# Second RMS norm of a decoder layer: squares behind the output projection, token-major sums, and the first FFN blocks by k tile

## The chip, the core and the metric

The kernel runs on one core of a Trainium2 chip. The metric is the time of the whole kernel on the device, in microseconds (us), median of several runs. Engines: TensorE (PE in the profile, its weight loads PEld), VectorE (DVE), ScalarE (ACT), GpSimd (POOL), and SyncE (SP), which here issues most of the DMAs. TensorE's clock has two levels, 1.2 and 2.4 GHz; the profile gives the granted clock as a share of the higher.

## The reference

One layer of a hybrid decoder trunk, on x of 1024 tokens by 1024 channels, float32. What matters here is the end of the layer:

```
mixed = (gate_a * o_a + gate_b * o_b + gate_c * o_c) @ w_out
x  = x + g1 * mixed
h2 = rms_norm(x) * (1 + sc2) + sh2          # x * rsqrt(mean(x*x, over channels) + 1e-6)
gate, up = split(h2 @ w_ffn_in, 2)          # D_FF = 2816
x  = x + g2 * ((silu(gate) * up) @ w_ffn_out)
```

Before it stand a first adaLN norm, one wide input projection and three branches (RG-LRU, RWKV-7, sliding-window attention), which the change doesn't touch.

## The kernel before

**Layout.** Activations are channel-major: a k tile is 128 channels on the partitions and 1024 tokens in the free dimension, so x is eight k tiles (`x2`). The names T and D are 1024, KT is 8, P is 128. Sums over channels are sums over partitions and over k tiles, and are done by TensorE.

**Dense products.** Every matrix product runs on float32 split in two parts, high and low: weights in `w_hi`, `w_lo`, activations in `x_hi`, `x_lo`. `dense` takes one block, 128 output channels: for each k tile `three_passes` issues hi*hi, hi*lo, lo*hi on two halves of 512 tokens, six matmuls (L246). A block's result lies in two of the eight PSUM banks, chosen by its slot (0 or 1; banks 0 and 1, or 2 and 3). The weights of all blocks form one stream with two slots. SP loads a block's raw weights (`load_block`, L228) once the block two before it has been split. POOL splits it (`split_block`, a cast at L236 and a subtraction at L238) once the raw weights have landed and the block two before, which has the same slot, is done on TensorE. TensorE waits for the split.

**Order.** No planner: each engine runs its own written program in order, and semaphores join them. A helper `upto(n)` turns "n events done" into a wait. SP's queue is in order too, so a load that waits holds back every load written behind it.

**The merge and x.** The last branch product (`ob1`) leaves the merged activations in `mix`; ScalarE rounds them to `x_hi` (L1349), VectorE makes `x_lo` (L1830). x, which comes token-major from memory, is loaded again in eight tiles of 128 tokens into two slots of `yraw` (L580 to L585) and transposed by TensorE (L1025 to L1031) into banks 4 to 7, two banks for each parity of the tile; ScalarE copies each into `x2` (L1353). SP issues the load of tile t once tile t-2 has been transposed, and only behind tile 7's load come the loads of w_out.

**wout.** Sixteen blocks, two halves of four k tiles. After each block VectorE adds g1 times the result into `x2` (L1838, the residual). Behind the second half the tiles of x are final one by one.

**The second norm.** ScalarE squares tile k into one of two buffers `mt` (L1359); TensorE multiplies a 128x128 matrix of ones with it, so that all 128 rows of banks 4 and 5 hold the sums of every token (L1044), in its program behind all of wout. ScalarE waits for the sums of tile k-2 before it squares tile k. Then ScalarE takes the root of 128x1024 (L1361) and VectorE the reciprocal (L1843). Per tile: VectorE scales (L1847), ScalarE adds the shift and rounds to `x_hi` (L1364), VectorE makes `x_lo` (L1850), and only then scales the next tile.

**The FFN.** A block pair (gate and up) for each 128 hidden channels. The first block, ffn_first's gate, follows the ladder tile by tile (`ready`), the second comes after it. ScalarE takes silu of the gate block (L1370), VectorE the product with the up block (L1856); ScalarE and VectorE split the hidden tile (L1374, L1861), and every two tiles a down projection follows. Then comes the loop over the other pairs.

## Time and profile before

| | |
|---|---|
| median of 3 runs | 3149.4 us (3149.35 to 3154.89) |
| profiled execution | 3150.6 us, span 3148.8 us |
| mean granted clock of TensorE | 0.964 |
| TensorE busy | 2926.4 us, 93% of the span |
| VectorE busy | 1458.6 us, 46% |
| ScalarE busy | 706.7 us, 22% |
| GpSimd busy | 724.0 us, 23% |

The profile is of one execution. Its time points count from the start of the span. TensorE's matmuls are pipelined and their ends are modelled, so a start to start distance tells more than a duration. An engine's idle time is put down to what ended it; idle time of an engine off the chain of work costs nothing.

### The profile page before, as it was taken

Reading aid. Unit: us, or ns where it says so; the run is one execution under the profiler, and the core shown is the slowest. Engines: PE = TensorE matmul, PEld = TensorE weight load, DVE = VectorE, ACT = ScalarE, POOL = GpSimd, SP = SyncE. Lnnn points to the kernel's source line nnn. Section 1 sums busy time; section 2 is a strip of 40 time slices with the busy share of each in tenths; the row PEclk is TensorE's granted clock in tenths of the full one; section 3 lists DMA queues with packets and bytes.
Section 4 is the critical chain, followed back from the end, with each engine's and each line's share of the span. In section 5 each row is a group of like instructions: output and inputs, shape, how many; then the busy total and the mean of one; then the engine's idle time right before and its main releaser. Section 6 shows DMA issues by size and latency. Waiting matters only on the chain.

```text
span 3148.8 us, 61688 instructions
## 1 busy us (share of the span) xinstructions
PE 2926.4 (93%) x25715; PEld 2385.0 (76%) x25715; DVE 1458.6 (46%) x1801; ACT 706.7 (22%) x1004; POOL 724.0 (23%) x454
## 2 busy tenths in 40 slices
PE   1899999999999999999979988989897999999998
PEld 1687878787888888776757766777685888888886
DVE  6555454555454554675744655445523222222222
ACT  1222121212121221244435664001202000000001
POOL 0212020203021111132312101333231333333331
PEclk7999999999999999999989998999897999999999
DMA  5111111102010110233421102333410111111111
GB/s 179 49 44 35 37 42 31 54 19 70 23 50 29 44 36 29 78 109 88 124 64 38 44 14 83 115 122 128 134 54 27 47 47 53 47 47 47 53 47 67
DMA packets 247066, 192.75 MB, mean 61 GB/s; under 512 B 21729, under 2 KB 225083, under 8 KB 246843
## 3 DMA queue, kind: packets, MB, share of 16 engines
q1 hardware_dynamic: 239136, 163.02, 17.5%
q10 hardware_dynamic: 7707, 26.34, 2.1%
q8 instruction: 191, 3.13, 0.4%
q14 instruction: 32, 0.26, 0.0%
HBM read 158.91 MB, written 30.41 MB: 60 GB/s over the span
## 4 chain that ended last, share of the span: by engine, by line
PE 84%; DVE 8%; ACT 4%; issue 3%; DMA 1%; ACTq 0%; DVEq 0%; POOL 0%; SPq 0%; POOLq 0%
PE ps L246 59%; PE ps L772 2%; PE ps L786 2%; PE ps L783 2%; PE ps L750 2%; DVE arena L1424 2%; PE ps L835 1%; PE ps L866 1%; PE ps L867 1%; PE ps L952 1%; PE ps L977 1%; PE ps L965 1%; DVE arena L1649 1%; PE ps L720 1%; ACT arena L1275 1%
## 5 line engine op out<-in xcount | busy, mean ns | idle before, releaser
L246 PE MATMUL ps<-x_hi,w_hi 128*128 128x512 f32 (+1 forms) x2576 | 839.5, 401 | 49.9 <-DVE x_lo L1850 17.7
L246 PE MATMUL ps<-x_lo,w_hi 128*128 128x512 f32 (+1 forms) x2576 | 821.8, 395 | 0.0
L246 PE MATMUL ps<-x_hi,w_lo 128*128 128x512 f32 (+1 forms) x2576 | 820.0, 394 | 0.0
L236 POOL CAST w_hi<-w_raw 128x1024 fp32r<-128x1024 f32 (+2 forms) x221 | 224.1, 1014 | 2365.4 <-PE ps L246 1629.4
L246 PEld LDWEIGHTS ps<-x_hi,w_hi 128*128 128x128 f32 (+1 forms) x2576 | 485.1, 191 | 189.6 <-issue 66.1
L246 PEld LDWEIGHTS ps<-x_hi,w_lo 128*128 128x128 f32 (+1 forms) x2576 | 489.6, 190 | 106.7
L246 PEld LDWEIGHTS ps<-x_lo,w_hi 128*128 128x128 f32 (+1 forms) x2576 | 490.9, 191 | 104.4
L238 POOL TENSOR_TENSOR w_lo<-w_raw,w_hi 128x1024 fp32r<-128x1024 f32 (+2 forms) x221 | 484.2, 2191 | 17.7
L1856 DVE TENSOR_TENSOR arena<-ps,arena 128x1024 f32<-128x1024 f32 x22 | 26.9, 1225 | 396.3 <-PE ps L246 396.3
L1873 DVE SCALAR_TENSOR_TENSOR arena<-ps,mod,arena 128x1024 f32<-128x1024 f32 x88 | 113.0, 1284 | 129.1 <-PE ps L246 129.1
L1591 DVE COPY_PREDICATED arena<-hid_lo,ps 128x256 f32<-128x256 int32 x144 | 72.0, 500 | 139.8 <-PE ps L783 90.4
L1424 DVE SCALAR_TENSOR_TENSOR arena<-arena,mod 128x128 f32<-128x128 f32 (+1 forms) x280 | 129.0, 461 | 10.0
L1374 ACT ACTIVATE hid_hi<-arena 128x1024 fp32r<-128x1024 f32 x22 | 23.4, 1062 | 450.7 <-PE ps L246 316.9
L246 PE MATMUL ps<-hid_hi,w_hi 128*128 128x512 f32 x352 | 109.1, 391 | 4.8 <-DVE hid_lo L1861 4.8
L246 PE MATMUL ps<-hid_lo,w_hi 128*128 128x512 f32 x352 | 108.8, 390 | 0.0
L246 PE MATMUL ps<-hid_hi,w_lo 128*128 128x512 f32 x352 | 108.8, 390 | 0.0
L1275 ACT ACTIVATE arena<-arena 128x256 f32<-128x256 f32 x128 | 75.4, 591 | 84.4 <-DVE arena L1754 84.4
L786 PE MATMUL ps<-arena 64*64 64x64 f32 x2560 | 89.4, 218 | 0.0
L1504 DVE TENSOR_TENSOR arena<-arena 128x1024 f32<-128x1024 f32 (+1 forms) x27 | 42.9, 1588 | 98.3 <-ACT arena L1120 97.3
L772 PE MATMUL ps<-arena 64*64 64x64 f32 x2560 | 84.5, 218 | 0.7
L786 PEld LDWEIGHTS ps<-arena 64*64 64x64 f32 x2560 | 83.2, 135 | 0.2 <-issue 0.2
L772 PEld LDWEIGHTS ps<-arena 64*64 64x64 f32 x2560 | 80.2, 135 | 1.7 <-issue 1.6
(263 smaller groups left out, 3541.5 us busy)
## 6 DMA issues: line engine op xcount, KB each, us to landing
w_raw<-in_w_in SPq DMA_DIRECT2D x78, 512.0 KB, 3.9
w_raw<-in_w_ffn_in SPq DMA_DIRECT2D x44, 512.0 KB, 3.8
arena<-in_w_ada SPq DMA_DIRECT2D x32, 512.0 KB, 3.8
gates_sig<-arena ACTq DMA_DIRECT2D x24, 512.0 KB, 2.6
arena<-gates_sig SPq DMA_DIRECT2D x24, 512.0 KB, 3.4
w_raw<-in_w_ffn_out SPq DMA_DIRECT2D x22, 512.0 KB, 3.5
arena<-in_x SPq DMA_DIRECT2D x16, 512.0 KB, 5.1
arena<-in_w_ada SPq DMA_DIRECT2D x8, 1024.0 KB, 12.0
```

Source lines behind the costliest of these rows:

```text
L236: nc.gpsimd.tensor_copy(hi, raw).then_inc(s_whi, 1)
L238: nc.gpsimd.tensor_tensor(lo, raw, hi.bitcast(F32), ALU.subtract).then_inc(s_wsplit, 1)
L246: ins = nc.tensor.matmul(dst[h], wp, xp[h], start=first and m == 0, stop=last and m == 2)
L750: ins = mm(dst, src[hp, c * CHUNK:(c + 1) * CHUNK], ar[hp, c, :, :], start=True, stop=True)
L772: ins = mm(bank(B, 2, hp)[:, c % BATCH, :], am[hp, c, AM_BA, :], xx[hp, 0, c, :], start=True, stop=True)
L783: ins = mm(bank(B, 0, hp)[:, c % BATCH, :], xx[hp, 1, c, :], y1[hp, c, :], start=True, stop=True)
L786: ins = mm(bank(B, 1, hp)[:, c % BATCH, :], y1[hp, c, :], xx[hp, 1, c, :], start=True, stop=True)
L1275: fn(sc[:, h, nn, :], sc[:, h, nn, :], ACT.Exp, bias=sm[:, SM_NEG, h, nn:nn + 1], scale=rq[:, gg % 2, t, n0 + nn, h:h + 1], accum_out=sm[: ...
L1424: ins = v.scalar_tensor_tensor(acc, w[:, k, :], c_k, acc, ALU.mult, ALU.add)
L1504: v.tensor_tensor(dst, x0, x1, ALU.subtract).then_inc(v_mix, 1)
L1591: v.copy_predicated(blocks_of(xx[:, o, batch(B), :], lv, o), level_mask(lv, o), blocks_of(bank(B, o), lv, o)).then_inc(v_xu, 1)
L1873: v.scalar_tensor_tensor(r, ps[:, 4 + 2 * (m % 2):6 + 2 * (m % 2), :], mod[:, MOD_G2 + m:MOD_G2 + m + 1], r, ALU.mult, ALU.add).then_inc(m ...
```

## The change

x is loaded into four slots instead of two (`x_in`: two new places in the arena and the two of `yraw`), so that the load of tile t waits for the transposes of tile t-4. ScalarE squares the final tiles of x while wout's second half is still running, tile 0 into an accumulator (`x2_acc`) and the others into the two buffers; VectorE adds tiles 1 to 5 to the accumulator between its residuals. TensorE then multiplies each 128x128 block of the accumulator and of the squares of tiles 6 and 7 (as weights) with one column of ones: 24 products that leave the sums token-major, 8 blocks of tokens in columns, a token on a partition. VectorE adds the three, ScalarE takes the root and VectorE the reciprocal of 128x8. To bring the factor back to channel-major rows, VectorE scales the identity by each of the eight columns (`x2_diag`) and TensorE multiplies ones with the eight results, into banks 6 and 7, which VectorE reads in the scaling of each tile (`normed`). VectorE scales tile k+1 before it makes `x_lo` of tile k. TensorE's first two FFN blocks are interleaved by k tile.

```diff
--- before.py
+++ after.py
@@ -405,19 +405,21 @@
         t_rc, t_n, t_d, t_p, t_z, t_dc = made_by("dve", "head_rsqrt", "k_normed", "softmax_steps", "probs_ready", "att_zeroed", "denominator_steps")
 
 
-        mg = carve([("x2", KT * T), ("mix", KT * T), ("gt", 2 * T), ("t", 2 * T), ("pad", 1536), ("yraw", 2 * T)])
+        mg = carve([("x2", KT * T), ("mix", KT * T), ("gt", 2 * T), ("t", 2 * T), ("pad", 1536), ("yraw", 2 * T), ("more", T)])
         assert 20 * T + 1536 >= 12296 + 6 * T + 3 * 9 * P and LRU_ARENA <= ARENA
         x2 = mg["x2"].rearrange("p (k n) -> p k n", k=KT)
         mix = mg["mix"].rearrange("p (k n) -> p k n", k=KT)
         yraw = mg["yraw"].rearrange("p (s n) -> p s n", s=2)
+        x_in = [mg["pad"][:, 0:T], mg["more"], yraw[:, 0, :], yraw[:, 1, :]]
         gtl = mg["gt"].rearrange("p (s n) -> p s n", s=2)
         mt = mg["t"].rearrange("p (s n) -> p s n", s=2)
+        x2_acc, x2_diag = gtl[:, 0, :], gtl[:, 1, :].rearrange("p (b n) -> p b n", b=8)
         s_y = [sem("y_tile_loaded_0"), sem("y_tile_loaded_1")]
         s_g = [sem("gate_tile_loaded_0"), sem("gate_tile_loaded_1")]
-        s_x2, s_out = [sem("x_loaded_again_0"), sem("x_loaded_again_1")], sem("out_stored")
+        s_x2, s_out = [sem(f"x_loaded_again_{k}") for k in range(4)], sem("out_stored")
         m_hi, m_sq, m_rt, m_sil, m_hh, m_o = made_by("act", "operand_high", "x2_squared", "x2_root", "silu_ready", "hidden_high", "out_copied")
-        m_lo, m_ev, m_xt, m_res, m_n, m_nh, m_act, m_hl, m_dn = made_by(
-            "dve", "operand_low", "merge_steps", "xT_ready", "residual_ready", "x2_rstd", "h2_steps", "hidden_ready", "hidden_low", "down_added")
+        m_lo, m_ev, m_xt, m_res, m_n, m_xn, m_nh, m_act, m_hl, m_dn = made_by(
+            "dve", "operand_low", "merge_steps", "xT_ready", "residual_ready", "x2_norm_steps", "h2_scaled", "h2_ready", "hidden_ready", "hidden_low", "down_added")
         m_pe, m_ss, m_dd, m_op = made_by("pe", "xT_done", "x2_sums_done", "down_done", "out_transposed")
 
 
@@ -578,11 +580,13 @@
                     load_y(g + 1, part)
 
             for t in range(8):
-                if t < 2:
+                if t >= 4:
+                    sp.wait_ge(m_pe, upto(t - 3))
+                elif t >= 2:
                     sp.wait_ge(m_lo, upto(NY))
                 else:
-                    sp.wait_ge(m_pe, upto(t - 1))
-                sp.dma_start(yraw[:, t % 2, :], a["x"][0, t * P:(t + 1) * P, :]).then_inc(s_x2[t % 2], 16)
+                    sp.wait_ge(t_oc, upto(ALL))
+                sp.dma_start(x_in[t % 4], a["x"][0, t * P:(t + 1) * P, :]).then_inc(s_x2[t % 4], 16)
             for half in range(2):
                 wv = a["w_out"][0][half * 512:(half + 1) * 512, :]
                 with sp.Fori(0, 4) as i:
@@ -1023,11 +1027,11 @@
                         dense(pe, Block(nm, c, i), tiles=kts, first=HALF * (g % 2), ready=(m_lo, Y0[g], 1))
 
             for t in range(8):
-                pe.wait_ge(s_x2[t % 2], 16 * (t // 2 + 1))
+                pe.wait_ge(s_x2[t % 4], 16 * (t // 4 + 1))
                 if t >= 2:
                     pe.wait_ge(m_xt, upto(t - 1))
                 for k in range(KT):
-                    ins = pe.transpose(ps[:, 4 + 2 * (t % 2) + k // 4, (k % 4) * P:(k % 4 + 1) * P], yraw[:, t % 2, k * P:(k + 1) * P], ident)
+                    ins = pe.transpose(ps[:, 4 + 2 * (t % 2) + k // 4, (k % 4) * P:(k % 4 + 1) * P], x_in[t % 4][:, k * P:(k + 1) * P], ident)
                 ins.then_inc(m_pe, 1)
             for half in range(2):
                 first = (HALF * (len(BR) % 2) + HALF * half) % KT
@@ -1038,16 +1042,24 @@
                         pe.wait_ge(m_res, upto(half * 8 + i * 2 + c - 1))
                         dense(pe, Block(f"wout{half}", c, i), tiles=HALF, first=first, ready=(m_lo, NY + HALF * half, 1))
 
-            for k in range(KT):
-                pe.wait_ge(m_sq, upto(k + 1))
-                for h in range(2):
-                    ins = mm(ps[:, 4 + h, :], ones, mt[:, k % 2, h * 512:(h + 1) * 512], start=k == 0, stop=k == KT - 1)
-                ins.then_inc(m_ss, 1)
-
-            def up(blk_gate, blk_up, tile, ready=None):
+
+            for n, sq in enumerate((x2_acc, mt[:, 0, :], mt[:, 1, :])):
+                if n == 0:
+                    pe.wait_ge(m_n, upto(5))
+                else:
+                    pe.wait_ge(m_sq, upto(KT - 2 + n))
+                for b in range(8):
+                    ins = mm(ps[:, 4, n * 8 + b:n * 8 + b + 1], sq[:, b * P:(b + 1) * P], ones[:, 0:1], start=True, stop=True)
+            ins.then_inc(m_ss, 1)
+            for b in range(8):
+                pe.wait_ge(m_n, upto(8 + b))
+                ins = mm(ps[:, 6 + b // 4, b % 4 * P:(b % 4 + 1) * P], ones, x2_diag[:, b, :], start=True, stop=True)
+            ins.then_inc(m_ss, 1)
+
+            def up(blk_gate, blk_up, tile):
 
                 pe.wait_ge(m_sil, upto(tile))
-                dense(pe, blk_gate, ready=ready)
+                dense(pe, blk_gate)
                 pe.wait_ge(m_act, upto(tile))
                 dense(pe, blk_up)
 
@@ -1069,7 +1081,17 @@
                         x = [[t[:, k, h * 512:(h + 1) * 512] for h in range(2)] for t in (hid_hi, hid_lo)]
                         ins = three_passes(dst, w, x, k == 0, k == FF_GROUP - 1)
                     ins.then_inc(s_dense if m % 4 == 3 else m_dd, 1)
-            up(Block("ffn_first", 0), Block("ffn_first", 1), 0, ready=(m_nh, 0, 2))
+            first_two = [Block("ffn_first", part) for part in range(2)]
+            for blk in first_two:
+                pe.wait_ge(s_wsplit, upto(blk.before + 1))
+            for k in range(KT):
+                pe.wait_ge(m_nh, upto(k + 1))
+                for blk in first_two:
+                    w = [t[:, blk.slot, k * P:(k + 1) * P] for t in (w_hi, w_lo)]
+                    x = [[t[:, k, h * 512:(h + 1) * 512] for h in range(2)] for t in (x_hi, x_lo)]
+                    ins = three_passes([ps[:, 2 * blk.slot + h, :] for h in range(2)], w, x, k == 0, k == KT - 1)
+                    if k == KT - 1:
+                        ins.then_inc(s_dense, 1)
             with pe.Fori(0, TURNS["ffn"]) as i:
                 up(Block("ffn", 0, i), Block("ffn", 1, i), i * 2 + 1)
                 up(Block("ffn", 2, i), Block("ffn", 3, i), i * 2 + 2)
@@ -1354,13 +1376,13 @@
 
             for k in range(KT):
                 act.wait_ge(m_res, upto(KT + k + 1))
-                if k >= 2:
-                    act.wait_ge(m_ss, upto(k - 1))
-                fn(mt[:, k % 2, :], x2[:, k, :], ACT.Square).then_inc(m_sq, 1)
-            act.wait_ge(m_ss, upto(KT))
-            fn(halves(yraw[:, 0, :]), ps[:, 4:6, :], ACT.Sqrt, scale=1.0 / D, bias=eps_rms).then_inc(m_rt, 1)
+                if k >= 3:
+                    act.wait_ge(m_n, upto(min(k - 2, 5)))
+                fn(x2_acc if k == 0 else mt[:, k % 2, :], x2[:, k, :], ACT.Square).then_inc(m_sq, 1)
+            act.wait_ge(m_n, upto(6))
+            fn(rstd, sumsq, ACT.Sqrt, scale=1.0 / D, bias=eps_rms).then_inc(m_rt, 1)
             for k in range(KT):
-                act.wait_ge(m_nh, upto(2 * k + 1))
+                act.wait_ge(m_xn, upto(k + 1))
                 fn(x_hi[:, k, :], mt[:, k % 2, :], ACT.Identity, bias=mod[:, MOD_SH2 + k:MOD_SH2 + k + 1]).then_inc(m_hi, 1)
 
             def hidden(blk, tile, t):
@@ -1829,25 +1851,43 @@
                 dve.wait_ge(m_hi, upto(NY + m + 1))
                 v.tensor_tensor(x_lo[:, at, :], mix[:, m, :], x_hi[:, at, :].bitcast(F32), ALU.subtract).then_inc(m_lo, 1)
             dve.wait_ge(m_xt, upto(8))
-            for half in range(2):
-                with dve.Fori(0, 4) as i:
-                    for c in range(2):
-                        blk = Block(f"wout{half}", c, i)
-                        dve.wait_ge(s_dense, upto(blk.before + 1))
-                        r = halves2(x2[:, bass.ds(i * 2 + c, 1), :])
-                        v.scalar_tensor_tensor(r, pair_of(blk.slot), mod[:, bass.ds(i * 2 + (MOD_G1 + c), 1)], r, ALU.mult, ALU.add).then_inc(m_res, 1)
-                dve.wait_ge(m_res, upto(8 * half + 8))
-
-            rs = yraw[:, 0, :]
+            def residual(half, i, c):
+
+                blk = Block(f"wout{half}", c, i)
+                dve.wait_ge(s_dense, upto(blk.before + 1))
+                r = halves2(x2[:, bass.ds(i * 2 + c, 1), :])
+                v.scalar_tensor_tensor(r, pair_of(blk.slot), mod[:, bass.ds(i * 2 + (MOD_G1 + c), 1)], r, ALU.mult, ALU.add).then_inc(m_res, 1)
+            with dve.Fori(0, 4) as i:
+                for c in range(2):
+                    residual(0, i, c)
+            dve.wait_ge(m_res, upto(8))
+            for m in range(KT):
+                residual(1, m // 2, m % 2)
+                if 2 <= m < 7:
+                    dve.wait_ge(m_sq, upto(m))
+                    dve.wait_ge(m_n, upto(m - 2))
+                    v.tensor_tensor(x2_acc, x2_acc, mt[:, (m - 1) % 2, :], ALU.add).then_inc(m_n, 1)
+            dve.wait_ge(m_ss, upto(1))
+            v.tensor_reduce(sumsq, ps[:, 4, 0:24].rearrange("p (s b) -> p b s", s=3), AX.X, ALU.add).then_inc(m_n, 1)
             dve.wait_ge(m_rt, upto(1))
-            v.reciprocal(rs, rs).then_inc(m_n, 1)
-            dve.wait_ge(m_n, upto(1))
+            v.reciprocal(rstd, rstd).then_inc(m_n, 1)
+            dve.wait_ge(m_n, upto(7))
+            for b in range(8):
+                v.tensor_scalar(x2_diag[:, b, :], ident, rstd[:, b:b + 1], None, ALU.mult).then_inc(m_n, 1)
+
+            def normed(k):
+
+                v.scalar_tensor_tensor(halves(mt[:, k % 2, :]), halves(x2[:, k, :]), mod[:, MOD_SC2 + k:MOD_SC2 + k + 1], ps[:, 6:8, :], ALU.mult, ALU.mult).then_inc(m_xn, 1)
+
+            dve.wait_ge(m_ss, upto(2))
+            normed(0)
             for k in range(KT):
-                t = mt[:, k % 2, :]
-                v.scalar_tensor_tensor(t, x2[:, k, :], mod[:, MOD_SC2 + k:MOD_SC2 + k + 1], rs, ALU.mult, ALU.mult).then_inc(m_nh, 1)
-                dve.wait_ge(m_nh, upto(2 * k + 1))
+                if k + 1 < KT:
+                    if k >= 1:
+                        dve.wait_ge(m_nh, upto(k))
+                    normed(k + 1)
                 dve.wait_ge(m_hi, upto(NY + KT + k + 1))
-                v.scalar_tensor_tensor(x_lo[:, k, :], t, mod[:, MOD_SH2 + k:MOD_SH2 + k + 1], x_hi[:, k, :].bitcast(F32), ALU.add, ALU.subtract).then_inc(m_nh, 1)
+                v.scalar_tensor_tensor(x_lo[:, k, :], mt[:, k % 2, :], mod[:, MOD_SH2 + k:MOD_SH2 + k + 1], x_hi[:, k, :].bitcast(F32), ALU.add, ALU.subtract).then_inc(m_nh, 1)
 
             def product(blk, tile, t):
 
```

## Rows read from the trace of the kernel before

**Rows 1.** The page's first part, busy time and share of the span
```profile
PE 2926.4 (93%) x25715; PEld 2385.0 (76%) x25715; DVE 1458.6 (46%) x1801; ACT 706.7 (22%) x1004; POOL 724.0 (23%) x454
```

**Rows 2.** Chain that ended last, 2230 to 2450: start, us, what
```profile
2267.19 3.83 DMA w_raw<-in_w_out
...
2273.48 89.67 PE ps L246 x384
2363.15 13.75 PE ps L1044 x32
...
2378.14 6.56 DVE arena L1843
...
2415.01 35.21 PE ps L246 x147
```

**Rows 3.** Timeline, x loads and transposes: start, us, engine, line, operation
```profile
2243.99 22.78 SPq L585 DMA_DIRECT2D arena<-in_x  x8
...
2257.19 2.86 PE L1030 MATMUL ps<-keep,arena 128*128 128x128 f32 x16 [4.42 <-ACT arena L1353]
...
2264.45 1.97 PE L1030 MATMUL ps<-keep,arena 128*128 128x128 f32 x8 [0.59 <-DMA arena<-in_x]
```

**Rows 4.** Stretches: length, TensorE (two: all engines) busy, clock, DMA share, GB/s
```profile
78.00:80.00 2.00, 1.84 (x10) 0.50 0.00 0
80.00:82.00 2.00, 0.95 (x7) 0.92 0.00 0
...
2278.00:2279.00 1.00, 1.00 (x5) 0.83 (x4) 0.00 (x0) 0.00 (x0) 0.00 (x0) 0.74 0.00 0
...
2380.00:2381.00 1.00, 0.00 (x0) 0.96 0.00 0
...
2388.70:2415.00 26.30, 20.47 (x42) 12.80 (x42) 17.25 (x14) 9.32 (x8) 0.00 (x0) 0.50 0.00 0
...
2418.00:2419.00 1.00, 1.00 (x4) 0.77 0.00 0
```

**Rows 5.** Timeline, last residual to third FFN block
```profile
2363.41 1.28 DVE L1838 SCALAR_TENSOR_TENSOR arena<-ps,mod,arena 128x1024 f32 x1 [4.23 <-PE ps L246]
...
2373.55 1.06 ACT L1359 ACTIVATE arena<-arena 128x1024 f32<-128x1024 f32 x1 [0.66 <-PE ps L1044]
...
2384.72 1.28 DVE L1847 SCALAR_TENSOR_TENSOR arena<-arena,mod 128x1024 f32<-128x1024 f32 x1
...
2388.74 1.19 PE L246 MATMUL ps<-x_hi,w_hi 128*128 128x512 f32 x2 [11.85 <-DVE x_lo L1850]
...
2418.11 1.04 POOL L236 CAST w_hi<-w_raw 128x1024 fp32r<-128x1024 f32 x1 [51.32 <-PE ps L246]
2419.23 2.40 POOL L238 TENSOR_TENSOR w_lo<-w_raw,w_hi 128x1024 fp32r<-128x1024 f32 x1
...
2428.97 0.62 PE L246 MATMUL ps<-x_hi,w_hi 128*128 128x512 f32 x2
```

**Rows 6.** Attention's head sums: a run in the timeline; a microsecond of another
```profile
1863.55 3.73 PE L936 MATMUL ps<-keep,arena 128*128 128x2 f32 x32
...
1668.00:1669.00 1.00, 1.00 (x6) 1.00 (x7) 0.00 (x0) 0.00 (x0) 0.00 (x0) 0.50 0.24 29
```

**Rows 7.** Groups by shape, small operations: count, busy us, mean ns, idle before
```profile
L1253 ACT ACTIVATE arena<-arena,bias_t 128x8 f32<-128x8 f32 x4 | 1.2, 301 | 2.6 <-DVE arena L1717 2.5
...
L1421 DVE TENSOR_SCALAR arena<-arena,mod 128x128 f32<-128x128 f32 x32 | 11.2, 350 | 9.1 <-DMA arena<-in_w_ada 9.0
...
L1438 DVE TENSOR_SCALAR arena<-arena,small 128x1024 f32<-128x1024 f32 x8 | 6.0, 753 | 0.3
...
L1436 DVE RECIPROCAL small<-small 128x8 f32<-128x8 f32 x1 | 0.2, 203 | 1.3 <-ACT small L1108 1.3
```

**Rows 8.** Timeline of the first norm, VectorE's steps from PSUM, two in succession
```profile
83.21 1.34 DVE L1456 TENSOR_SCALAR arena<-ps,mod 128x1024 f32<-128x1024 f32 x1
...
85.79 1.34 DVE L1456 TENSOR_SCALAR arena<-ps,mod 128x1024 f32<-128x1024 f32 x1
```

## The prediction

> **What bounds the kernel now.** I read the page first: TensorE is busy for 93% of the span, more than any other engine, so an edit pays where it takes TensorE time away or shortens a stretch in which TensorE waits [rows 1]. Then the chain of work over the stretches that the diff touches [rows 2]: it is TensorE's wout products from 2273.48 for 89.67 us, and around them two holes. The first (wout can't start) ends with a load of w_out. The second begins with the sums of squares (13.75 us), goes on through a reciprocal of 6.56 us and ends in a three-engine ladder that feeds the first FFN block one k tile at a time; the reader is to see that none of this is matmul at full rate. Third, the timeline of the two holes, for who starts when [rows 3, 5]. Last, the granted clock around them, since TensorE comes out of each hole at the lower level [rows 4].
>
> **Part 1, x in four slots.** All time points are before's. SP issues in order, and the w_out loads stand behind the x loads. Before, the load of x tile 7 waits for the transposes of tile 5, which end at 2264.45 + 1.97 = 2266.42 [rows 3]; the first w_out load is issued at 2267.19 and lands 3.83 us later [rows 2], POOL splits it, and wout begins at 2273.48: 7.06 us from tile 5's end. After, the load of tile 7 waits for tile 3 only. Tiles 2 and 3 are transposed from 2257.19 for 2.86 us, to 2260.05; their start waited for a ScalarE copy, not for a load [rows 3], so it stays. The same 7.06 us from there give 2267.1. TensorE must also have transposed tiles 4 to 7: eight transposes take 1.97 us at the lower clock, some 1.7 from start to start without the last one's tail (an estimate), so 2260.05 + 4 x 1.7 = 2266.9. Both come out alike. Gain 2273.48 - 2267.1 = 6.4; three x tiles and two weight blocks now lie closer together on the queues, so I take 6.3, with 5.5 as the low bound (late by half of the 1.7) and 6.4 as the high one. The eight loads still start at 2243.99 [rows 3], four at once, some 7 us before the first transposes; tiles 2 and 3 have 13 us. Nothing else is moved past them.
>
> **The clock at wout's start.** Before, it stood at 0.50 (1.2 GHz) until the slice 2278:2279 [rows 4], so wout's first 4.8 us ran at half rate and lost 2.4. After, TensorE transposes without a gap from 2257.2 for at least 6 us. In the first norm such a run did raise the clock: 0.50 in 78:80 with TensorE busy 1.84 of the 2 us, 0.92 in 80:82 [rows 4]. So I count on wout beginning at 2.4 GHz: gain 2.4, lower end 0. wout's rate at full clock is (89.67 - 2.4) / 384 = 0.227 us a matmul [rows 2].
>
> **Part 2, sums of squares.** Removed: 32 matmul instructions of 512 columns, alternating with six ScalarE squares, 13.75 us [rows 2]; the reciprocal over 1024 columns, 6.56 us. Moved: ScalarE squares all tiles behind wout's second half. Added to VectorE there: five adds of 128x1024, about 1.28 us each by the neighbouring residual; a wout block lasts 24 x 0.227 = 5.4 us and VectorE was idle for 4.2 us before its residual [rows 5], so an add fits, even at twice the price if POOL's split slows it. If the cover were gone, 5 x 1.28 = 6.4 us would come back.
> The last residual starts at 2363.41 and takes 1.28; its square (1.06) ends at 2365.8 [rows 5]. ScalarE's table load for the root has nothing to wait for and lies beside the sums. TensorE needs 24 products, 48 instructions, with one moving column. The attention's head sums are the same form with two columns: 32 in 3.73 us at the higher clock, 0.117 each; at the lower, 6 in a microsecond, 0.167 [rows 6]. The first 32 (the sum of six squares, and the seventh) can start at 2363.0. At 0.117: 2363.0 + 5.6 = 2368.6. But the clock does not outlive wide products for long: it was 0.50 in a slice full of narrow products [rows 6], and before it fell at the end of 2380:2381, 4.1 us after TensorE's last sum (2363.15 + 13.75 = 2376.9) [rows 2, 4]. So the last third runs partly at 0.167; I take 2368.9. Bounds: 2368.6, and 2363.0 + 48 x 0.167 = 2371.0.
> The Trainium skill ("TensorE: Matmul & The Clock Gate", "Back-to-back issue gap") gives products of 1 to 64 columns about 60 cycles at 2.4 GHz, 25 ns. By that figure the sums would end just behind the last square, near 2366.3, and my total would be 2.6 us shorter; the rows, in which each instruction has its own weight load, show 117 ns.
>
> **From the sums to the first product.** Reduce of 128x24, root and reciprocal on 128x8: 0.2 (an estimate, as the reciprocal), 0.30, 0.20 [rows 7], with about 0.1 us of handing over each: 2369.9. Eight scalings of the identity, 128x128: between 0.20 (eight columns) and 0.35; on the line from 0.20 to 753 ns for 1024 columns, 0.26 [rows 7]. They pace 2.1 us, but TensorE, at the lower clock again, spreads them by 16 instructions of 128 columns, twice the transposes' 1.7 us for eight: 2370.2 + 3.4 + 0.3 of tail = 2373.9 for the first h2 step. Bounds 2372.4 (higher clock) and 2376.0 (late sums). Before, it began at 2384.72 [rows 5]: gain 10.8. From that step to the first FFN matmul it is 2388.74 - 2384.72 = 4.0 us [rows 5], and stays so, since x_lo of tile 0 stands behind the step of tile 1, which fills the time of ScalarE's rounding. First FFN matmul at 2377.9.
>
> **Part 3, first two blocks by k tile.** Before, 2388.74 to the third block's start at 2428.97: 40.2 us [rows 5]. After, VectorE runs two instructions per tile without waiting for ScalarE. The first norm has this pattern (a step from PSUM, then x_lo) and repeats each 2.58 us [rows 8]. TensorE has 12 matmuls per tile: 2.7 us at 0.227, 5.4 at half clock. It starts slow, so it isn't starved, and the clock rises, as it did 4.8 us after 2273.48 and 3.2 us after the ladder's last gap (2415.01, then 2418:2419) [rows 2, 4]; take 4 us, which cost 2.0: 96 x 0.227 + 2.0 = 23.8 us (23.4 to 24.2). Both blocks end at 2401.7.
> New wait: the third block's weights go into slot 0, whose split on POOL waits for block 0, which now ends only 6 matmuls (1.4 us) before block 1. Before, that split hid under block 1. POOL starts some 0.3 us behind block 0, at 2400.6, and needs 1.04 + 0.08 + 2.40 = 3.5 us [rows 5], TensorE sees it 0.3 later: 2404.4, a stall of 2.7 us. Queued behind it are only the third block and what follows; silu hides in it, and the raw weights were loaded long before. The fourth block's split ends 3.5 us later, far ahead of need. Gain of the part: 40.2 - (2404.4 - 2377.9) = 13.7.
>
> **Sum.** 6.3 + 2.4 + 10.8 + 13.7 = 33.2 us. The profiled execution took 3150.6 (span 3148.8), so 3117.4; the median of the runs, 3149.4, is 1.2 below the profiled one, which gives 3116.2. I say 3117.
>
> **Rivals.**
> A, the clock isn't up at wout's start: 3117 + 2.4 = 3119. For: tile 7's load, issued at 2260.1, is needed by 2265.2, and the w_out load took 3.83 us, so it is tight. Against: gapless transposes raised it once.
> B, VectorE paces the joint blocks. It binds only from some 3.1 us a tile on. The ladder's tiles, (2415.01 - 2388.74) / 7 = 3.75 us with ScalarE in between, are the upper bound: 7 x 3.75 + 2.7 = 29.0 instead of 23.8, 3122. Against: 2.58 in rows 8.
> C, the clock falls in the new stall: half rate for 4.8 us again, 2.4 us, 3119. Against: it fell only 4.1 us after work stopped. The Trainium skill's same page ("A second HAM failure mode: psum-queue depth-cycling") says that small idles between groups of matmuls can make the clock swing; no row of before shows it for one gap of 2.7 us.
> D, the x loads bring nothing (w_out isn't freed early, or tiles 0 to 3 at once delay those behind): 3117 + 8.7 = 3126.
> E, narrow products cost far less than the rows say, the sums end at 2366.3: 3114.
> F, the other side: after the stall the FFN stays at 1.2 GHz. Each microsecond so spent loses 0.5; with 33.2 / 0.5 = 66 us of it the gain is gone, 100 us give 3167. For: through the ladder the clock stayed low for 26.3 us with TensorE busy for 20.5 of them [rows 4]. Against: the FFN's loop has no such gaps.
> A change that does nothing isn't possible here: the removed 13.75 and 6.56 us are on the chain.
>
> **Chances.** Forecast 0.52, A 0.18, B 0.07, C 0.07, D 0.07, E 0.04, F 0.05 (0.03 slower, 0.02 within). A measurement of this kernel tells about 0.2% (6.3 us) from no change: faster 0.95, same 0.02, slower 0.03. The range 3112 to 3124 takes in the forecast with its bounds (the higher clock in the spreading, 1.5; the sums' 0.3 below and 2.1 above; the loads' 0.8), A, C, most of B, and E; it leaves out D and F.
>
> **What would show it.** wout starting 6 us earlier after the attention's last product, at clock 1.00; eight squares inside wout; 48 narrow instructions in 5.5 to 6.5 us; the h2 steps 10 to 12 us after the last wout matmul instead of 21.6; TensorE without gaps over 96 matmuls; then one gap of 2.7 us before POOL's split is done. I am wrong if the small chain takes far over 5 us or the joint blocks are starved.

## The result and the profile after

| | before | after |
|---|---|---|
| median (range) of six runs each | 3151.8 us (3138.2 to 3156.9) | 3131.2 us (3121.8 to 3133.3) |
| profiled execution | 3150.6 us, span 3148.8 | 3130.6 us, span 3128.7 |

The ratio is 0.9933, with an interval of 0.991 to 0.9956: 20.6 us by the medians. The kernel became faster, but by less than the 33.2 us of the forecast and outside its range (3112 to 3124).

The first part of the page of after, for the same thing as [rows 1]:

```profile
PE 2925.8 (94%) x25747; PEld 2390.7 (76%) x25747; DVE 1459.3 (47%) x1815; ACT 706.5 (23%) x1004; POOL 726.0 (23%) x454
```

TensorE's busy time over the whole span hardly fell (0.6 us), but that sum hides two things that cancel. By stretch (its ends, length, TensorE busy, clock, DMA share, GB/s), first of before from its first transpose of x to its third FFN block:

```profile
2250.86:2428.97 178.11, 150.48 (x577) 0.84 0.19 56
```

and of after, between the same two marks:

```profile
2260.56:2409.17 148.61, 133.04 (x610) 0.92 0.20 59
```

There TensorE is busy for 17.4 us less (32 wide matmuls left, 48 narrow and 16 of 128 columns came, and more of the rest runs at the higher clock) and idle for 12.1 us less. Ahead of the first transpose of x it is busy for 16.0 us more, with the same instructions. The chain of after over the changed part, for comparison with [rows 2] (start, us, what):

```profile
2266.89 3.20 PE ps L1034 x16
...
2270.85 4.85 DMA w_raw<-in_w_out
...
2278.19 88.63 PE ps L246 x384
2366.82 7.22 PE ps L1052 x48
...
2375.20 3.80 PE ps L1056 x16
2379.02 2.47 DVE arena L1880 x2
2381.51 1.30 DVE x_lo L1890
...
2382.94 22.55 PE ps L246 x90
...
2405.67 1.01 POOL w_hi L236
...
2406.77 2.35 POOL w_lo L238
...
2409.17 40.87 PE ps L246 x179
```

Every step of the forecast is in it: the load of w_out behind the transposes of tile 3, narrow sums in place of 13.75 us of wide ones, no long reciprocal, 96 matmuls nearly in one piece, then a wait for POOL's split. But wout starts at 2278.19, 4.7 us *later* than before's 2273.48, where 6 us earlier was forecast. To see why, the transposes of x in the two traces (min/median/max ns, first and last start). Of before:

```profile
L1030 PE MATMUL ps<-keep,arena x64: 270/421/477, 2250.9 to 2271.7; 128*128 128x128 f32 x64
```

Of after:

```profile
L1034 PE MATMUL ps<-keep,arena x64: 270/273/421, 2260.6 to 2275.7; 128*128 128x128 f32 x64
```

The first transpose stands 9.7 us later in the trace of after, and no instruction of TensorE, VectorE, ScalarE or GpSimd ahead of it was changed. From there on the stretches can be compared, whatever came before (the tail behind the third FFN block is 719.2 to 720.6 us in all traces):

| stretch, us | before | after | gain | forecast |
|---|---|---|---|---|
| first transpose of x to wout | 22.6 | 17.6 | 5.0 | 6.3 |
| wout | 89.67 | 88.63 | 1.0 | 2.4 |
| wout's end to the first h2 step | 21.57 | 12.20 | 9.4 | 10.8 |
| h2 step to first FFN matmul | 4.0 | 3.9 | 0.1 | 0 |
| first FFN matmul to third block | 40.24 | 26.23 | 14.0 | 13.7 |
| all | 178.1 | 148.6 | 29.5 | 33.2 |

29.5 gained, less the 9.7 by which the stretch ahead was longer, plus 0.3 of tail: 20.1, the difference of the two spans.

### The profile page after: what moved, and what is told of

Read it like the earlier page. It is cut to its first block, busy times and chain, and to the rows that moved or that the text cites. A ratio compares the mean times of both kernels' runs of the same rounds, so it can differ in the third digit from the quotient of the medians.

```text
span 3128.7 us, 61733 instructions
## 1 busy us (share of the span) xinstructions
PE 2925.8 (94%) x25747; PEld 2390.7 (76%) x25747; DVE 1459.3 (47%) x1815; ACT 706.5 (23%) x1004; POOL 726.0 (23%) x454
## 3 DMA queue, kind: packets, MB, share of 16 engines
q1 hardware_dynamic: 239136, 163.02, 17.6%
## 4 chain that ended last, share of the span: by engine, by line
PE 84%; DVE 8%; ACT 4%; issue 3%; DMA 1%; ACTq 0%; DVEq 0%; POOL 0%; SPq 0%; POOLq 0%
PE ps L246 59%; PE ps L776 2%; PE ps L790 2%; PE ps L787 2%; PE ps L754 2%; DVE arena L1446 1%; PE ps L839 1%; PE ps L870 1%; PE ps L871 1%; DVE arena L1671 1%; PE ps L956 1%; PE ps L981 1%; PE ps L969 1%; PE ps L724 1%; PE ps L723 1%
## 5 line engine op out<-in xcount | busy, mean ns | idle before, releaser
L1896 DVE TENSOR_TENSOR arena<-ps,arena 128x1024 f32<-128x1024 f32 x22 | 26.9, 1225 | 392.8 <-PE ps L246 392.8
L1581 DVE TENSOR_TENSOR arena<-ps,arena 128x1024 f32<-128x1024 f32 x8 | 9.8, 1225 | 166.4 <-PE ps L698 166.4
L790 PEld LDWEIGHTS ps<-arena 64*64 64x64 f32 x2560 | 83.4, 135 | 0.4 <-issue 0.3
```

The source lines that it names most:

```text
L790: ins = mm(bank(B, 1, hp)[:, c % BATCH, :], y1[hp, c, :], xx[hp, 1, c, :], start=True, stop=True)
```

## The experiments

For each kernel the traces give the same marks: x0, the first transpose of x; the *region*, from x0 to the third FFN block; and the time of the RWKV loop ahead, from the start of its turn 1 to that of turn 8. "Before" beside a kernel means the kernel before on the same chip.

### The same kernels once more

`before_again` and `after_again` are the two kernels unchanged.

> The kernel before, unchanged, for a second profile of the part ahead of the change. In the first profiles the attention's last product ended (TensorE's first x transpose) at 2250.9 us before and at 2260.6 after, though the program up to there is the same. Theory U (chance): in the RWKV loop of eight turns, TensorE's clock falls in some turns behind a run of single-column products, in 3 clock dips before and 7 after up to 1300 us, each 3 to 5 us long in cost; where the dips fall differs from execution to execution, so this profile may show the first x transpose anywhere from 2245 to 2265. Theory V (the change slows it): this profile shows 2251 again, within 1.5 us. Both: from the first x transpose to the start of the third FFN block 178 us, as in the first profile.

> The changed kernel, unchanged, to narrow the interval and for a second profile. Theory U: the stretch from the first x transpose to the third FFN block takes 148.6 us as before (within 2), the stretch ahead of it varies by several us with the number of clock dips in the RWKV loop, and in a mean over executions the gain tends to the 29.5 us of the changed stretch minus what chance leaves. Theory V: the first x transpose at 2260.6 again, within 1.5 us, and the total gain 20 us, ratio 0.9935.

| | span | RWKV | x0 | region |
|---|---|---|---|---|
| before (first) | 3148.8 | 1014.2 | 2250.9 | 178.1 |
| before_again | 3156.9 | 1024.9 | 2257.6 | 179.3 |
| after (first) | 3128.7 | 1021.9 | 2260.6 | 148.6 |
| after_again | 3136.6 | 1030.1 | 2268.0 | 148.9 |
| after_again_2 | 3137.8 | 1027.7 | 2269.6 | 148.3 |

Timed: after_again 3131.9 against 3157.2 before, ratio 0.9917 [0.9883, 0.9952]. x0 moves by up to 9 us between traces of one kernel, the region by about 1. Executions of before ranged over 3146 to 3176 here (23 of them), more than five times the width of the three shown ahead of the prediction.

What lengthens the loop is seen by the clock. Turn 4 has 64 products of a 64x64 matrix with one column, then wider ones, then the dense product. The timeline of after (start, us, engine, line):

```profile
600.79 2.03 PE L719 MATMUL ps<-keep,arena 64*64 64x1 f32 x64
602.75 1.12 PE L723 MATMUL ps<-arena 128*128 128x512 f32 x2
603.81 1.12 PE L724 MATMUL ps<-arena 32*128 32x512 f32 x2
604.86 1.87 PE L723 MATMUL ps<-arena 128*128 128x512 f32 x2
606.66 2.07 PE L724 MATMUL ps<-arena 32*128 32x512 f32 x2
```

The pair of L724 takes 1.12 us the first time and 2.07 the second. The stretches behind it, of after (length, TensorE busy, clock, DMA share, GB/s):

```profile
605.00:611.00 6.00, 6.00 (x10) 0.51 0.32 87
```

and of before, the same microseconds:

```profile
605.00:611.00 6.00, 6.00 (x21) 1.00 0.32 87
```

TensorE is busy all 6 us in both, with the same DMA traffic; but at 1.2 GHz it issues 10 matmuls, at 2.4 GHz 21. In these two traces a turn with such a dip lasts 146.5 to 148.1 us, one without 142.6 to 145.3. Before's first trace had two behind the single-column products of the eight turns, after's had six. That gave two theories: U, the dips are chance, and come behind the single-column products; V, the change itself brings them.

### Wide products in the loop

`before_wide` and `after_wide` give those products 64 columns; nothing reads the 63 others, and the output is the same. In both:

```diff
-ins = mm(ps[hp, 4, c:c + 1], rw["bv"][hp, c * CHUNK:(c + 1) * CHUNK], ones[hp, 0:1], ...)
+ins = mm(ps[hp, 4, c:c + 64], rw["bv"][hp, c * CHUNK:(c + 1) * CHUNK], ones[hp, 0:64], ...)
```

> The kernel before, with the 64 single-column products of each RWKV turn made 64 columns wide (the moving operand is ones, each product writes its own column and columns that the next one overwrites; the result is the same). Theory U says that the clock dips of the RWKV loop start behind these narrow products. If they are the trigger, the dips between 300 and 1300 us vanish, the loop's turns are 143.3 us each, and the first x transpose stands near 2244 (2251 less three dips, plus 8 x 0.4 us for the wider products), executions scatter less, and the total is 5 to 12 us below the kernel before. Theory U': the dips come from the low activity of the whole passage (the products with 32 rows behind it too) and stay; then no change beyond +3 us. Theory V has no reason for a change.

> The same widening on the changed kernel. Theory U: the first x transpose at the same time as in the kernel before with the widening, within 2 us (if the widening works), and the total 29 to 30 us below that kernel, which is what the changed stretch gains in the traces. Theory V: the first x transpose 9 us later than there, total only 20 us below it.

One execution of after_wide took 5799 us, for no reason that the record shows, and is left out; three remain, 3106.1 to 3113.1. The loop's stretch of before and of before_wide, whose loop ends sooner:

```profile
310.00:1181.00 871.00, 847.61 (x13151) 0.99 0.13 39
```
```profile
310.00:1174.00 864.00, 840.03 (x13219) 1.00 0.13 40
```

After and after_wide:

```profile
310.00:1188.00 878.00, 855.33 (x13130) 0.98 0.13 39
```
```profile
310.00:1174.00 864.00, 840.09 (x13221) 1.00 0.13 40
```

With 64 columns the loop holds 2.4 GHz throughout and is equally long in both: 1005.0 and 1005.0 us. So the loop of after isn't slower by itself. This alone doesn't tell whether the change makes the dips more frequent. Two things speak against it. The dips vary with one and the same loop: three traces of after had six each, but lag2, one_after_other and acc7 below, whose loop is after's, had one, three and eight (the two plain traces of before had two and four). And on one chip the dips cost both kernels alike: by means, before less before_wide_2 is 21.5 us and after_again_2 less after_wide_3 20.9, each give or take 6. V is out as far as these executions can tell, and U stands. before_wide against before: 3138.5 against 3151.6, ratio 0.9962 [0.994, 0.9984], though TensorE does more work. Its executions also scatter less (standard deviation 2.5 to 3.7 us instead of about 9).

`before_wide_2`, `after_wide_2` and `after_wide_3` repeat them, `after_again_2` repeats the kernel after; all but after_wide_2 (and best, below) on one chip.

> The kernel before with wide products in the RWKV loop, on another chip. Theory U: below the kernel before by 10 to 20 us, executions within 10 us of each other, and 29 to 30 us above the changed kernel with the same widening. Theory V: 20 us above it.

> The changed kernel with the wide products again, to have enough executions beside those of the kernel before with the same widening (3138.5 us median, 12 executions within 9 us). Theory U: 3110, 28 to 30 us less than that, executions within 9 us of each other. Theory V: 3118.

> The changed kernel with wide products, beside before_wide_2 on the same chip. Theory U: 29 to 30 us below before_wide_2. Theory V: 20 us below. The changed stretch 148.5 us in the trace under both.

> The changed kernel unchanged, on this chip. Theory U: the dips cost both kernels alike in the mean, so that over all comparisons the gain lies between 25 and 30 us; a single comparison can be off by 5 us. Theory V: near 20 us again.

| | median (range), us | ratio to before |
|---|---|---|
| after_wide_2 (other chip) | 3116.9 (3115.9 to 3120.7) | 0.9849 [0.9825, 0.9873] |
| before_wide_2 | 3137.7 (3132.4 to 3139.7) | 0.9928 [0.9904, 0.9953] |
| after_wide_3 | 3110.9 (3106.0 to 3113.3) | 0.9846 [0.9818, 0.9873] |
| after_again_2 | 3130.8 (3121.4 to 3139.7) | 0.9908 [0.9877, 0.9938] |

With the dips gone from both, the change brings 26.4 ± 2.9 us here and 29.2 ± 4.4 in the first pair (differences of means; the second rests on only three executions of after_wide and is less certain than its figure says). The traces' regions say 28.1 to 28.6 (wide) and 29.5 (plain). The first comparison's 20.6 is low, but within its own interval (14 to 28 us); the plain kernels differed by 25 us in the two later ones. What stays of x0, 3.3 to 3.7 us later in after_wide than in before_wide, lies outside the loop. In the first pair it is between the attention's last head sum and x0, a stretch that is 379 to 387 us long in the traces of before and after alike (379.1 in before_again, 383.9 in both first traces, 387.1 in after_wide); in the second pair that stretch differs by only 0.6 (384.1 and 383.5), and the rest lies ahead of it in the attention. So these are other places of scatter. Their cause stays open, and so does whether a cost of the change of up to some 3 us is in them.

### Each half alone

`x_only` is before with the four slots for x; `norm_only` is after with x loaded into two slots as before:

```diff
-                if t >= 4:
-                    sp.wait_ge(m_pe, upto(t - 3))
-                elif t >= 2:
+                if t < 2:
                     sp.wait_ge(m_lo, upto(NY))
                 else:
-                    sp.wait_ge(t_oc, upto(ALL))
-                sp.dma_start(x_in[t % 4], ...
+                    sp.wait_ge(m_pe, upto(t - 1))
+                sp.dma_start(x_in[2 + t % 2], ...
```

> Part 1 alone on the kernel before: four slots for x, the norm and the FFN as before. In the profile of the changed kernel the stretch from the first x transpose to wout's first matmul was 17.6 us instead of 22.6, and wout took 88.6 instead of 89.7. Expected: 5.0 + 1.0 = 6 us less in the stretch from the first x transpose to the end of wout; the norm's stretch as before (66 us from wout's end to the third block). Total 6 us faster, 0.998, plus or minus what the part ahead does: theory U says it can be as much as 10 us either way, theory V says it depends on whether the arena's new place or the four semaphores are at fault: then the first x transpose is at 2260.

> Parts 2 and 3 alone: x in two slots as before, the new norm and the FFN blocks by k tile. Expected: the first x transpose to wout's end as before (112 us), from wout's end to the third FFN block 42.3 us instead of 65.8, 23.5 less. Total 23.5 us faster, 0.9925, again give or take the part ahead of it by theory U; by theory V the first x transpose at 2251 if x's slots and semaphores are what slows it, at 2260 if the length of the program is.

x_only 3151.3, 0.9973 [0.9946, 1.0]: as expected, but at the edge of what this comparison can tell from nothing. Its trace shows it: x0 to the second norm's first sum 106.6 us instead of 112.1, region 170.9. norm_only 3137.3, 0.9932 [0.9906, 0.9957], region 154.6, stretch to the first sum 112.1 as before. From before's 178.1 the halves take 7.2 and 23.5, together 30.7; the whole takes 29.5. They add up, and rival D is out.

### The joint blocks

`one_after_other` runs the two FFN blocks in turn instead of by k tile; `lag2` lets the second follow two k tiles behind the first:

```diff
-            for k in range(KT):
+            for k, blk in [(s - lag, blk) for s in range(KT + 2) for lag, blk in zip((0, 2), first_two) if 0 <= s - lag < KT]:
                 pe.wait_ge(m_nh, upto(k + 1))
-                for blk in first_two:
```

(one_after_other has `[(k, blk) for blk in first_two for k in range(KT)]` there.)

> The changed kernel with the first two FFN blocks one after the other, the first following the h2 steps. Only the stretch from the first FFN matmul to the third block counts: 26.2 us in the changed kernel (22.6 of products, 3.6 to the third block's start behind the split). The first block is paced by VectorE, 7 x 2.6 us + 6 matmuls = 20 us, the second adds 10.9, the third follows without a stall: 31 us, 5 us more than interleaved. If VectorE's pace weren't hidden in the interleaved form the difference would be smaller; if the split's stall ate the gain, the two would be alike.

> The changed kernel with the second block two k tiles behind the first, so that 18 matmuls (4.1 us) follow the first block's last and cover the split of the third block's weights (0.3 + 1.0 + 0.1 + 2.4 + 0.3). If the stall between the second and the third block (2.3 us between matmuls in the changed kernel) is POOL's split and nothing else, it vanishes: 24.0 us from the first FFN matmul to the third block instead of 26.2. If the early tiles starve TensorE (its clock rises while it waits for the third tile), 24.5 to 25. A rival: another wait is behind the stall, then 26.2 stays.

From the first FFN matmul to the third block: 26.2 in after, 28.8 in one_after_other, 24.1 in lag2. Of the 14.0 us that this part brings, the sequence by k tile accounts for 2.5, less than the 5 expected: VectorE ended the last tile 16.2 us behind the first FFN matmul, not 18.2. The rest, by subtraction, is mostly the ladder without ScalarE in it: 2.51 us a tile instead of 3.75, 8.7 us over seven tiles; some 3 us are not told apart. In after POOL ends the split at 2406.77 + 2.35 = 2409.12 and TensorE idles 2.33 us for it; in lag2 the timeline has no idle time of TensorE there:

```profile
2384.13 1.04 POOL L236 CAST w_hi<-w_raw 128x1024 fp32r<-128x1024 f32 x1 [32.44 <-PE ps L246]
...
2385.25 2.40 POOL L238 TENSOR_TENSOR w_lo<-w_raw,w_hi 128x1024 fp32r<-128x1024 f32 x1
...
2387.87 0.62 PE L246 MATMUL ps<-x_hi,w_hi 128*128 128x512 f32 x2
```

The stall's cause is thus the split, as forecast, and it is avoidable. (one_after_other, lag2, acc7 and warm were timed once each: 3128.1, 3109.1, 3155.6 and 3139.3 us. With one to eight dips in them, these totals tell nothing of the change; only their regions count.)

### The sums and the clock at wout's start

`acc7` adds the square of tile 6 to the accumulator too, before the last residual, so that 32 narrow instructions are left (16 of them behind the last square); `warm` gives TensorE four discarded products in its gaps ahead of wout:

```diff
+                if m == 7:
+                    dve.wait_ge(m_sq, upto(7))
+                    dve.wait_ge(m_n, upto(5))
+                    v.tensor_tensor(x2_acc, x2_acc, mt[:, 0, :], ALU.add).then_inc(m_n, 1)
                 residual(1, m // 2, m % 2)
...
-            for n, sq in enumerate((x2_acc, mt[:, 0, :], mt[:, 1, :])):
+            for n, sq in enumerate((x2_acc, mt[:, 1, :])):
```
```diff
                 ins.then_inc(m_pe, 1)
+                if t == 6:
+                    pe.wait_ge(m_ev, upto(EV_ALL))
+                for _ in range({6: 1, 7: 3}.get(t, 0)):
+                    mm(ps[:, 0, 0:C_KEEP], ones, keep[:, :], start=True, stop=True)
```

> The changed kernel with the square of tile 6 too added to the accumulator by VectorE, so that TensorE takes 16 products (32 instructions) instead of 24 (48) for the sums. In the traces of the changed form 48 instructions took 6.8 to 7.2 us from wout's end. The accumulator's 8 products can run from wout's end at once (1.9 us at 0.117), tile 7's 8 only behind its square, 2.9 us behind wout's end, and take 1.9 more: sums done 5.0 us behind wout's end, against 7.1, and the first FFN matmul 2 us earlier (14 us behind the first sum instead of 16). If the narrow products cost as little as the 25 ns figure, nothing changes, since the last square would already set the end.

> The changed kernel with discarded 384-column products of constants behind the transposes of x tile 6 (one) and tile 7 (three), in the gap in which TensorE waits for w_out's split; the first wout product overwrites their bank. If the missing 1.3 us of wout's start are the clock alone (it stood at 0.50 for the first 2.7 us of wout), wout's 384 matmuls take 87.3 to 87.6 us instead of 88.6 to 88.9, and start at the same time (17.2 to 17.8 us behind the first transpose), or up to 0.5 us later. If the clock doesn't follow such fillers, 88.6 stays.

Regions 148.4 and 148.0, against after's 148.3 to 148.9: neither is worth anything that counts alone. In acc7 the stretch from the first sum to the FFN is 14.0 instead of 16.3, but the first sum comes 1.1 later and the joint blocks take 1.0 more, so that the expected 2 us are gone. The chain of acc7 shows the first (L1868 is the new add, L1859 the last residual):

```profile
2387.89 1.23 DVE arena L1873
...
2389.21 3.23 DVE arena L1868
2392.44 1.21 DVE arena L1859
2394.78 2.88 PE ps L1052 x16
```

The new add took 3.23 us beside POOL's subtraction; the last residual and TensorE's first sum (2392.5) waited for it. warm has wout at full clock, 87.31 us instead of 88.63, but then its sums take 8.04 instead of 7.22, since they run longer at the lower clock, and its joint blocks 27.1.

### All together

`best` has lag2, the wide products, acc7 and warm; `best_2` repeats it on another chip, beside after_wide_3.

> All four together on the changed kernel: wide products in the RWKV loop, the second FFN block two tiles behind, the seventh square added, the fillers. Against the changed kernel with the wide products: 2.3 (stall) + 2 (sums) + 1.2 (clock) = 5 us less in the changed stretch, 143 us from the first x transpose to the third FFN block; total 3105, ratio to the kernel before 0.985. If the gains don't add (the FFN's start waits for VectorE), 145 us.

> The combined version again: 5 to 8 us below after_wide_3 (5.6 us by the changed stretch, 148.5 less 142.9; 7.6 by the medians of the last comparison).

best 3109.3 (3106.1 to 3110.4), 0.9824 [0.9803, 0.9845]; best_2 3104.0 (3102.7 to 3110.9), 0.9831 [0.9803, 0.9858]. That is faster than both kernels, and 6.9 to 7.6 us below after_wide on the same chip. The region is 142.9, 5.7 less than in after: lag2's 2.7, and another 3 that acc7 and warm bring here and did not bring alone (12.8 from the first sum to the FFN, with joint blocks of 24.6). Whether they need lag2 for it, or only each other, no run tells.

## Why the prediction was right and wrong

**Right in direction and mechanism, wrong in the number.** The forecast said 3117; it came to 3131.2. Of these 14.2 us, 3.7 are terms that were sized too large, and about 10 come from the level that was taken for the part ahead of the change.

**The step that failed** is "All time points are before's", and with it "the profiled execution took 3150.6 ..., so 3117.4". The arithmetic took one execution's level, and three runs within 5.5 us, as the level of the kernel. In the profiled execution of after the RWKV loop ran through more dips of the clock (its last narrow product starts at 1190.1 instead of 1183.2) and the stretch from there to x0, in which the last of the six dips falls, was 2.8 longer: x0 9.7 us later. The wide kernels show no part of the change in it that the noise would let one see. If either level was unusual, it was before's: the changed kernel came to 3131.2, 3131.9 and 3130.8 in its three comparisons, while before, 3149.4 in the three runs ahead of the prediction, had medians of 3151.6 to 3166.5 in the four later ones. The difference that the change makes, 26 to 29.5 us, would have given 3121 to 3125 from the profiled 3150.6, around the upper end of the range; and the range had no term for the scatter of the part that isn't changed.

**x in four slots, 6.3; measured 5.0.** wout followed tile 3's transposes as forecast. The load of w_out took 4.85 us instead of the 3.83 of [rows 2], with x tiles on the queues at the same time, and the second pair of transposes 3.20 instead of 2.86; the low bound, 5.5, had left too little for that.

**The clock at wout's start, 2.4; measured 1.0.** Rival A, for the most part. Stretches of after:

```profile
2267.40:2270.80 3.40, 3.40 (x19) 0.50 0.36 113
2277.00:2278.00 1.00, 0.00 (x0) 0.82 0.00 0
2278.00:2281.00 3.00, 2.81 (x7) 0.50 0.29 87
2281.00:2283.00 2.00, 2.00 (x10) 0.99 0.48 139
```

The transposes without a gap did raise the clock, but tile 7's came late, TensorE idled 1.24 us before them and 2.22 behind them, and just ahead of wout's first product the clock fell, for 3 us (before: 4.8). That warm gets 87.31, against 384 x 0.227 = 87.2, shows that this was the whole of wout's loss. But it bought little, since 0.8 of the 1.3 us was lost again in the sums and 0.9 in the joint blocks.

**The sums, 10.8; measured 9.4.** The spreading and the small steps hold to a tenth: from the reduction to the first h2 step 4.95 us, forecast 5.0. The term that was off is the 48 narrow instructions: 7.2 us instead of 5.9. In the stretches:

```profile
2366.00:2369.00 3.00, 3.00 (x26) 1.00 0.43 128
2369.00:2370.00 1.00, 1.00 (x10) 0.90 0.47 141
2370.00:2374.00 4.00, 4.00 (x19) 0.50 0.45 130
2374.00:2382.80 8.80, 3.81 (x17) 0.50 0.00 1
```

The clock fell after some 3 us of narrow products although TensorE was never idle; the forecast had them at 2.4 GHz for two thirds. From start to start, 29 of them took 0.112 each and 19 took 0.213, which make up the 7.2; the forecast had 0.117 and, for the lower clock, 0.167, read from one microsecond of [rows 6], too little. The Trainium skill ("TensorE: Matmul & The Clock Gate", "Back-to-back issue gap") gives about 25 ns as the gap between such products, weight loads not counted. This trace, in which each instruction has its own weight load, has 112 ns at the same clock, and rival E is out.

**The joint blocks, 13.7; measured 14.0.** TensorE paced them (76 matmuls in 17 us at full clock, 0.224 each), the clock rose some 4 us after the start, the stall was 2.33 for a forecast of 2.7. Rival B would have needed gaps. C is out: the clock stayed at 1.00 through the stall.

```profile
2382.80:2386.00 3.20, 3.06 (x7) 0.50 0.00 0
2386.00:2388.00 2.00, 2.00 (x8) 0.78 0.00 0
2388.00:2405.00 17.00, 17.00 (x76) 1.00 0.00 1
...
2405.00:2409.00 4.00, 1.83 (x9) 1.00 0.00 0
...
2420.00:3120.00 700.00, 693.41 (x3069) 1.00 0.15 47
```

With the last row, 700 us of FFN at 2.4 GHz, F is out too. What the Trainium skill says on the same page ("A second HAM failure mode: psum-queue depth-cycling") is about small idles that come back between the groups of matmuls; the one gap of 2.33 us here lowered nothing, while the idles of 1.24 and 2.22 us around eight short products ahead of wout did go with a fall.

## What to carry to other kernels

A forecast made as a difference holds better than one made as a level: compare the changed stretch from a mark of its own in both traces, and give the unchanged part a term for its scatter, taken from several executions. Where TensorE runs many products of one or two columns, look at the granted clock behind them; widening them, though it computes more, can be the faster and the steadier kernel. When two blocks end almost together and share a resource for the block after next (here the weight slots), let one run two tiles ahead.

## What the runs showed that I had not expected

- A busy TensorE can lose its clock. In the RWKV loop 64 single-column products took 2.0 us, and 2 us behind their end the clock was at 1.2 GHz in some turns, in others not, with the same instructions. With 64 columns no turn of any of the seven traces lost it, and before gained 13 to 18 us; without them the eleven others had one to eight dips. What decides in a given turn stays open.
- Gains at one level of the clock are partly given back. warm shortened wout by 1.3 and paid 0.8 in the sums and 0.9 in the joint blocks; acc7 cut a third of the narrow instructions and the first FFN products ran at 1.2 GHz for longer, 6.1 us instead of 4.0. The likely reason, only argued, is that TensorE did less ahead of them.
- VectorE's add of 128x1024 and GpSimd's subtraction seem to take turns. In after the add beside a split takes 2.0 us, and the one that began just ahead of GpSimd's 1.22, while that subtraction took 3.42 instead of 2.35:

```profile
2357.18 2.01 DVE L1869 TENSOR_TENSOR arena<-arena 128x1024 f32<-128x1024 f32 x1
...
2362.62 1.22 DVE L1869 TENSOR_TENSOR arena<-arena 128x1024 f32<-128x1024 f32 x1
2362.67 3.42 POOL L238 TENSOR_TENSOR w_lo<-w_raw,w_hi 128x1024 fp32r<-128x1024 f32 x1
```

  The subtraction ended 2.25 us behind the end of that add, nearly its 2.35 alone; the new add of acc7 ended 1.09 us behind the end of the subtraction (2387.93 + 3.42), nearly its 1.22 alone. Each looks as if it had waited for the other's end. The residual (1.28), of which some 0.5 us lie beside a subtraction, is not slowed by it. The forecast had priced the adds at up to twice 1.28 and found them covered; they were, five of them, and the sixth of acc7 was not.
